# The delta rule's preparation and the first loads in another order, with six unread products ahead of the first group's scores

## The reference

```
x = x + 0.5 * swiglu(rmsnorm(x, ffn1_norm[i]), ffn1_w_gu[i], ffn1_w_down[i])     # i = 0 is the program's start
q, k, v = silu(conv4(h @ w_qkv));  q, k = unit(q) / sqrt(128), unit(k)           # mixer of layers 0 and 3
beta = sigmoid(h @ w_b);  g = -exp(a_log) * softplus(h @ w_a + dt_bias)
G = cumsum(g) inside each tile of 128 tokens                                     # 2 tiles, 8 heads of 128
L[i,j]  = beta[i] * exp(G[i] - G[j]) * (k[i] . k[j])   for j < i
QK[j,i] = exp(G[i] - G[j]) * (q[i] . k[j])             for j <= i
u = (I + L)^-1 (beta * (v - decayed k @ S));   o = decayed q @ S + QK^T u;   S = decayed S + k^T u
```

## Time and profile before

| | |
|---|---|
| median of the three runs | 3758.79 us (3758.35 to 3759.87) |
| the profiled execution: its time, its span | 3753.71 us, 3752.0 us |
| PE busy | 3662.1 us (98%) |
| DVE, ACT, POOL busy | 2248.1, 1474.3, 270.2 us |
| mean granted clock of PE | 0.993 |
| moved by DMA | 660.51 MB, 176 GB/s in the mean |

### The profile page before, as it was taken

The page is one execution under the profiler, slowest core; times in us unless marked ns, Lnnn a source line. Parts: engine busy times, 40 slices in busy tenths (PEclk is TensorE's granted clock), DMA queues, the critical chain, the costliest instruction groups (busy, mean ns, idle before and its releaser), DMA issues.

```text
span 3752.0 us, 47545 instructions
## 1 busy us (share of the span) xinstructions
PE 3662.1 (98%) x18612; PEld 3030.6 (81%) x18612; DVE 2248.1 (60%) x2973; ACT 1474.3 (39%) x1957; POOL 270.2 (7%) x322
## 2 busy tenths in 40 slices
PE   7998999999999999999998999999999999999999
PEld 6898788889788875888898788888888688888587
DVE  5777577774577755777776577555434555541254
ACT  3454244443434424444462344444311444431143
POOL 0003200000000001000013100000001100000000
PEclk9999999999999999999999999999999999999999
DMA  8652086764476744766640374645532254553452
GB/s 291 234 171 85 20 278 213 246 230 152 158 250 207 259 145 152 241 233 225 221 149 26 134 264 159 223 146 202 164 100 66 81 202 168 202 196 101 168 179 102
DMA packets 453529, 660.51 MB, mean 176 GB/s; under 512 B 15288, under 2 KB 385299, under 8 KB 452904
## 3 DMA queue, kind: packets, MB, share of 16 engines
q1 hardware_dynamic: 432280, 579.48, 45.5%
q0 software_dynamic: 21072, 78.56, 6.5%
HBM read 656.94 MB, written 2.00 MB: 176 GB/s over the span
## 4 chain that ended last, share of the span: by engine, by line
PE 92%; DVE 4%; ACT 2%; issue 1%; SPq 0%; POOL 0%; DMA 0%; POOLq 0%; ACTq 0%; DVEq 0%
PE ps L790 14%; PE ps L792 14%; PE ps L791 14%; PE ps L810 7%; PE ps L812 7%; PE ps L811 7%; PE ps L1137 4%; PE ps L3080 3%; PE ps L800 2%; PE ps L1551 1%; PE ps L2800 1%; PE ps L2803 1%; DVE parts L727 1%; PE ps L3077 1%; PE ps L1483 1%; PE ps L1484 1%
## 5 line engine op out<-in xcount | busy, mean ns | idle before, releaser
L727 DVE TENSOR_TENSOR parts<-ring,parts 128x2048 fp32r<-128x2048 f32 (+1 forms) x339 | 756.9, 2235 | 609.4 <-ACT parts L713 609.3
L790 PE MATMUL ps<-parts 128*128 128x512 f32 x2288 | 905.3, 396 | 0.5 <-DVE parts L998 0.3
L792 PE MATMUL ps<-parts 128*128 128x512 f32 x2288 | 891.8, 390 | 0.0
L791 PE MATMUL ps<-parts 128*128 128x512 f32 x2288 | 890.9, 389 | 0.0
L713 ACT ACTIVATE parts<-ring 128x2048 fp32r<-128x2048 f32 x330 | 630.6, 1913 | 569.1 <-PE ps L792 417.3
L792 PEld LDWEIGHTS ps<-parts 128*128 128x128 f32 x2288 | 429.4, 188 | 91.4
L790 PEld LDWEIGHTS ps<-parts 128*128 128x128 f32 x2288 | 429.9, 188 | 85.9 <-issue 1.7
L791 PEld LDWEIGHTS ps<-parts 128*128 128x128 f32 x2288 | 430.2, 188 | 84.8
L810 PE MATMUL ps<-parts 128*128 128x512 f32 x1144 | 450.3, 394 | 0.3
L812 PE MATMUL ps<-parts 128*128 128x512 f32 x1144 | 446.1, 390 | 0.0
L811 PE MATMUL ps<-parts 128*128 128x512 f32 x1144 | 445.2, 389 | 0.0
(11 more groups left out here) (433 smaller groups left out, 4443.3 us busy)
## 6 DMA issues: line engine op xcount, KB each, us to landing
ring<-in_ffn_w_gu SPq DMA_DIRECT2D x176, 1024.0 KB
ring<-in_ffn_w_in SPq DMA_DIRECT2D x110, 1024.0 KB
ring<-in_ffn_w_down SPq DMA_DIRECT2D x88, 1024.0 KB
ring<-in_ffn_w_out SPq DMA_DIRECT2D x55, 1024.0 KB
ring<-in_gdn_w_in SPq DMA_DIRECT2D x32, 1024.0 KB
arena<-in_w_mod POOLq DMA_DIRECT2D x24, 1024.0 KB, 6.0
xn<-in_w_mod POOLq DMA_DIRECT2D x24, 1024.0 KB, 7.7
arena<-in_w_mod POOLq DMA_DIRECT2D x48, 512.0 KB, 9.1
```

What stands on the lines that cost most here:

```text
L727: ins = nc.vector.tensor_tensor(lower, unit_raw(at, j)[:, sides_, :], upper, ALU.subtract)
L790: nc.tensor.matmul(dst, h_u, w_u[:, :, n, :], start=(k == 0), stop=False)
L791: nc.tensor.matmul(dst, h_u, w_l[:, :, n, :], start=False, stop=False)
L792: ins = nc.tensor.matmul(dst, h_l, w_u[:, :, n, :], start=False, stop=(k == KD - 1))
```

## The change

Two places change: the start, and the preparation of both delta rules. At the start, constants are cut in 320 columns that go first and 3168 that go after chunk 2; the 14 small loads go to ACT's queue ahead of everything else ACT does; the other six go on SP behind chunk 2; ACT splits its first two units before `rows_act`; DVE makes their lower parts before it waits for `gains_ready`; PE makes 9 unread products in place of 12; and in the first feed-forward the first chunk's `up` calls go by half, then tile (the semaphore counts in `unit_freed` and `sums_done` follow). In the delta rule, PE's, ACT's and DVE's orders change, spread 1 goes to bank 3, six unread products precede group 0, and values, the decayed k and the small product move in among the level updates.

```diff
-    def rows_sp(sp):
+    def gain_rows_act(act):
...
+    def rows_sp(sp):
...
+    def late_consts_sp(sp):
+        sp.dma_start(consts[:, C_EARLY:NCONST], A["consts"][:, C_EARLY:NCONST]).then_inc(consts_loaded, 16)
@@ rows_dve
-        dve.wait_ge(gains_ready, 6)
@@ ffn_sp
             ffn_load(sp, at, c)
+            if c == RING - 1 and at is PLACES[0]:
+                rows_sp(sp)
+                late_consts_sp(sp)
@@ ffn_pe
-                spin(12, 3)
+                spin(9, 3)
-        up(0, 1, 0)
-        up(0, 0, 1)
-        up(0, 1, 1)
+        for half, t in ((0, 1), (1, 0), (1, 1)) if at is PLACES[0] else ((1, 0), (0, 1), (1, 1)):
+            up(0, half, t)
@@ ffn_act
-            rows_act(act)
             for j in range(GU_SLOTS):
                 gu_upper_act(act, at, j)
+            rows_act(act)
@@ ffn_dve
             split_first_dve(dve, at)
+            dve.wait_ge(gains_ready, 6)
@@ gdn
+    SPREAD = [7, 3, 7, 6]
+    PREP_SPREAD, PREP_GROUP = [1, 2, 3, 6], [4, 5, 7, 8]
@@ gdn_pe
         spread(0)
+        spread(1)
         to_rows(0)
         to_rows(1)
         turn(NQKV - 1)
         to_rows(2)
         to_rows(3)
-        spread(1)
+        spread(2)
+        spin(6, 2)
+        group(0)
         for n in range(4, 8):
             to_rows(n)
-        spread(2)
-        group(0)
+        group(1)
         spread(3)
-        for g in range(1, 4):
-            group(g)
+        wide_level(*SCHED[0])
+        group(2)
+        group(3)
@@ gdn_act
         silu_of(NQKV - 1)
+        table("natural_log_exp_and_others")
         to_rows(1)
-        table("natural_log_exp_and_others")
+        decay(0)
+        decay(1)
...
-        decay(0)
         for n in range(4, 8):
             to_rows(n)
-        for g in range(1, 4):
-            decay(g)
+        decay(2)
+        decay(3)
@@ gdn_dve
-        differences(0)
-        differences(1)
...
-        values(0)
...
-        differences(2)
...
-        nc.vector.tensor_tensor(k0, k0, bc_last(g_kd, P), ALU.mult).then_inc(gdn_kd, 1)
+        for g in range(3):
+            differences(g)
         group(0)
+        group(1)
         differences(3)
-        values(1)
-
-        group(1)
         update(*SCHED[0])
         group(2)
         group(3)
-        for t, lv in SCHED[1:-1]:
+        for n, (t, lv) in enumerate(SCHED[1:-1]):
             update(t, lv)
+            if n == 1:
+                values(0)
+            if n == 3:
+                keys()
+            if n == 5:
+                values(1)
```

More of the change, by code:

```diff
@@ L79 @@
 C_UPPER = 320
+C_EARLY = C_UPPER
 C_LOWER = 448
@@ L527, in spin @@
             nc.tensor.matmul(ps[:, bank, (c % 4) * P:(c % 4 + 1) * P], ident, col(C_ONES), start=True, stop=True)
[L529 removed]
+    def gain_rows_act(act):
         r = 0
         for name, rows in (("ffn1_norm", 4), ("mix_norm", 4), ("ffn2_norm", 4)):
[L532 removed]
+            act.dma_start(gain_rows[r:r + rows, :], A[name]).then_inc(gains_loaded, 16)
             r += rows
[L534 to L536 removed]
+        act.dma_start(gain_rows[r:r + 6, :], A["norm_g_2"].rearrange("l j d -> (l j) d")).then_inc(gains_loaded, 16)
+        act.dma_start(gain_rows[18:19, :], A["c_2"]).then_inc(gains_loaded, 16)
+        act.dma_start(gain_rows[19:20, :], A["c_ctx_2"].rearrange("(a d) -> a d", a=1)).then_inc(gains_loaded, 16)
         for j in range(2):
[L539 removed]
+            act.dma_start(col_rows[0:96, j, :], A["gdn_conv"][j].rearrange("w (c p) -> (w c) p", p=P))\
                 .then_inc(gains_loaded, 16)
@@ L543, in rows_sp @@
                 A[name].rearrange("l (c p) -> (l c) p", p=P)
-            sp.dma_start(col_rows[r:r + v.shape[0], 0, :], v).then_inc(gains_loaded, 16)
+            act.dma_start(col_rows[r:r + v.shape[0], 0, :], v).then_inc(gains_loaded, 16)
+        for l in range(2):
+            act.dma_start(m_rows[0:NMOD, l, :], A["b_mod_2"][l].rearrange("(n p) -> n p", p=P))\
+                .then_inc(gains_loaded, 16)
+    def rows_sp(sp):
         for j in range(2):
@@ L550, in rows_sp, with wait_all_consts @@
         sp.dma_start(d_gk[:, :], A["dsa_kidx_norm"][0].partition_broadcast(P)).then_inc(rows_loaded, 16)
-        for l in range(2):
-            sp.dma_start(m_rows[0:NMOD, l, :], A["b_mod_2"][l].rearrange("(n p) -> n p", p=P))\
-                .then_inc(gains_loaded, 16)
+    def late_consts_sp(sp):
+        sp.dma_start(consts[:, C_EARLY:NCONST], A["consts"][:, C_EARLY:NCONST]).then_inc(consts_loaded, 16)
+    def wait_all_consts(eng, at):
+        if at is MIXERS[0]:
+            eng.wait_ge(consts_loaded, 32)
     def rows_pe(pe):
@@ L690, in unit_freed @@
             j += UNITS[at["kind"]]
-        first = at["kind"] in ("ffn", "gdn") and j < 2
+        first = at["kind"] in ("ffn", "gdn") and j < 2 and at is not PLACES[0]
         return 2 * at["unit"] + (3 + j if first else 2 * j + 2)
     def sums_done(at, b, t):
-        return 2 * at["unit"] + (2 + 2 * t if b == 0 else 4 * b + 3 + t)
+        return 2 * at["unit"] + (2 + 2 * t if b == 0 and at is not PLACES[0] else 4 * b + 3 + t)
     def count(n, it, step):
@@ L1313, in gdn_pe @@
     def gdn_pe(pe, at):
+        wait_all_consts(pe, at)
         j = at["n"]
@@ L1422, in group @@
                 pe.wait_ge(gdn_conv, NQKV * (j + 1))
+                pe.wait_ge(gdn_D, 4 * j + hg + 1)
             else:
@@ L1489, in merge @@
                 ins.then_inc(gdn_TV, 1)
-        for t, lv in SCHED[:-1]:
+        wide_level(*SCHED[0])
+        group(2)
+        group(3)
+        for t, lv in SCHED[1:-1]:
             wide_level(t, lv)
@@ L1718, in gdn_dve @@
     def gdn_dve(dve, at):
+        wait_all_consts(dve, at)
         j = at["n"]
@@ L1757, in differences @@
             cols = slice(8 * t + 4 * hg, 8 * t + 4 * hg + 4)
-            dve.wait_ge(gdn_prep, 8 * j + (g + 1 if g < 3 else 5))
-            step(dve, nc.vector.tensor_tensor(wide(g_V[:, g, :]), wide(ps[:, 7 - g % 2, :]), bc_last(g_gc[:, cols], P),
+            dve.wait_ge(gdn_prep, 8 * j + PREP_SPREAD[g])
+            step(dve, nc.vector.tensor_tensor(wide(g_V[:, g, :]), wide(ps[:, SPREAD[g], :]), bc_last(g_gc[:, cols], P),
                                               ALU.subtract))
@@ L1840, in gdn_dve, with keys @@
                     unit(1)
-        differences(0)
-        differences(1)
-        dve.wait_ge(gdn_tok, NQKV * (j + 1))
-        values(0)
-        dve.wait_ge(gdn_gates, 6 * j + 6)
-        step(dve, nc.vector.scalar_tensor_tensor(out=g_nb, in0=g_beta[:, 8:16], scalar=-1.0, in1=g_eg[:, 8:16],
-                                                 op0=ALU.mult, op1=ALU.mult))
-        differences(2)
-        dve.wait_ge(gdn_Tps, 8 * j + 4)
-        k0 = g_tok[:, 0, D:2 * D].rearrange("p (h d) -> p h d", d=P)
-        nc.vector.tensor_tensor(k0, k0, bc_last(g_kd, P), ALU.mult).then_inc(gdn_kd, 1)
+        def keys():
+            dve.wait_ge(gdn_gates, 6 * j + 6)
+            step(dve, nc.vector.scalar_tensor_tensor(out=g_nb, in0=g_beta[:, 8:16], scalar=-1.0, in1=g_eg[:, 8:16],
+                                                     op0=ALU.mult, op1=ALU.mult))
+            dve.wait_ge(gdn_Tps, 8 * j + 4)
+            k0 = g_tok[:, 0, D:2 * D].rearrange("p (h d) -> p h d", d=P)
+            nc.vector.tensor_tensor(k0, k0, bc_last(g_kd, P), ALU.mult).then_inc(gdn_kd, 1)
+        for g in range(3):
+            differences(g)
         group(0)
+        group(1)
         differences(3)
-        values(1)
-        group(1)
         update(*SCHED[0])
@@ L1902, in gdn_pool @@
     def gdn_pool(pool, at):
+        wait_all_consts(pool, at)
         j = at["n"]
@@ L3543, in _ @@
             ffn_load(sp, PLACES[0], 0)
-            rows_sp(sp)
             for at in STEPS:
@@ L3550, in _ @@
         def _(act):
+            gain_rows_act(act)
             for at in STEPS:
```

18 lines of the change are left out of this document (7 added, 11 removed).

## The result

The changed kernel takes 3733.09 us in the median of four runs (3728.74 to 3734.00). The kernel before, run beside it on the same chip, took 3759.24. The ratio is 0.9928, with a 95% interval of 0.9911 to 0.9946, so it is faster by 0.5 to 0.9%. The forecast was 3739.3 with a range of 3731.5 to 3750: the time lies in the range, and the gain (26 us) is larger than the one forecast (19.5).

The account below looks back on a forecast made before the run. The prediction took PE as the bound, 92% of the chain, with gains only where the chain leaves PE or PE's time is not work. Start 8.2 plus preparation 11.3 gave 19.5: 3758.8 - 19.5 = 3739.3 us, range 3731.5 to 3750.

Parts of the forecast that it names:

- The start: Program start: first read product at 22.6 in place of 30.8, 8.2 us off, from 5 (ACT held) to 9.
- Chunk 0: First weights at the start: last byte at 16.2, under h's last copy at 17.9, so they would not delay it.
- The preparation: Both delta rules, first spread to third merge: 5.7 us off in each, 11.3 in both.
- the clock's term: Delta rule preparation: two to three low-clock stretches of PE, 1.6 us each, counted as 4.1 us lost.
- 9.8 - 4.1: Each delta rule: 9.8 us won up to the third merge less 4.1 for low clock, giving 5.7.
- Both gaps that the sum had named: PE's idle gaps left in the first delta rule's preparation: 341.8 to 344.9, with 0.45 of work within, and 354.7 to 356.9.
- The moved DVE work: `values` and `keys` moved into the delta rule's level loop: cost nothing, levels staying 5.4 us apart.
- the median of the runs lies 5.1 above that execution: Whole program: 5.1 us from profiled execution to median, taking the forecast from 3734.2 to 3739.3.
- A: Rival: delta rule preparation gives its gain back through clock falls or delays; 3750.6 us, chance 0.11.
- B: Rival: the start gains nothing, bound by transfers or ACT held by its issues; 3747.5 us, chance 0.08.
- C: Rival: slower, low clock lasting from group 2 in both delta rules; 12.4 us slower, 3771, chance 0.03.
- D: Rival: both places hidden by a stream that fixes the end; 3758.8 +- 4 us, chance 0.04.

Follow-up runs that it names:

- e8: The changed kernel with the 14 small loads issued by SP behind chunk 0 instead of by ACT; 3731.31 us, ratio 0.9936 to the kernel before.
- e3: The changed kernel run once more, unchanged; 3731.79 us, ratio 0.9919 to the kernel before.
- e11: The changed kernel with level 0 of tile 0 on PE back behind groups 2 and 3; 3748.04 us, ratio 0.9976 to the kernel before.
- e12: The new start with the old preparation, only level 0 of tile 0 moved between groups 1 and 2; 3742.62 us, ratio 0.9960 to the kernel before.
- e2: The kernel before with the delta rule's new preparation alone, old start kept; 3742.27 us, ratio 0.9950 to the kernel before.
- e1: The kernel before with the new start alone, delta rules left as before; 3749.54 us, ratio 0.9969 to the kernel before.

## Why the prediction was right, point by point

**The start.** The sum's steps and what the trace of after has: x lands by 6.8 (1.32 and 5.5 to landing; forecast 6.4); ACT's first square 7.37 (7.5); second transposes end 17.13 (17.25); h's last copy 17.77 (17.9); small rows turned 18.88 (19.05); unread products end 22.80 (22.65); first read product 22.46, or 22.81 in the chain, from which the forecast was reckoned (22.6). The estimate of 0.38 us for an issue on ACT's queue, which no row of before showed, was good: 14 issues took 5.2 us, 0.37 each, and in the eleven traces that have them there they end between 6.0 and 6.9. The two ends that the forecast gave the start, 5 us with ACT held and 9, rest on issues that hold ACT much longer or cost it nothing; no run shows either, only those 5.1 to 6.0 us. Behind the start chunks 1 and 2 were complete at 26.5 and 42.1 (26 and 40); ACT waited 0.41 us for chunk 2, and PE had no gap above 0.1 us from the first read product to 215 us. Chunk 0 was the step that came nearest to failing. The forecast had it by 16.2, of which 0.7 us is for the small loads ahead of it. e8, where they stand behind it, has it only at 17.2, 1.7 later than that sum without them (15.5); in the changed kernel its last transfer reports at 17.87, and ACT begins on it at 17.89. So nothing was left of the 1.7 us of cover counted, and had the norms been faster, the weights would have set the start.

The Trainium skill says in "DMA: Bandwidth & Descriptors", section "Issuing engines are not separate DMA queues", that transfers started by several engines interleave on the same 16 DMA engines. The runs agree, with numbers for this case: x lands 5.5 us after its issue with the 14 loads on ACT's queue and 4.9 with them behind chunk 0 (e8), so in this pair 0.26 MB of small loads cost it 0.6; the prediction's estimate by that page was 0.7. From run to run it varies as much: with the 14 loads on ACT's queue and the constants cut x took 5.3 to 6.2 us, and ACT's issues and table load still set the first square.

One price was missing. By their distances the passes were slow during the unread products before, too, but by the time 24 were over they had become fast. With 18 they had not: the first three read products stand at 22.46, 23.03 and 23.46, and only from 23.87 on are they 0.23 us apart. From the first to the fourth it takes 1.41 us where it took 0.82 before, so this costs 0.6 us. The fourth product is 7.62 us sooner than before (31.49 and 23.87), and so is the first spread (7.68), short of the 8.21 at the first.

**The preparation.** The path was right at nearly each mark, and the size of the clock's term was not. Distances from the first spread, forecast and (measured in e3, which had no low clock before merge 1): group 0 7.9 (8.1), group 1 12.0 (12.2), group 2 18.3 (18.6), merge 1 24.1 (24.5), merge 3 33.6 at full clock (34.8 with one low stretch). I counted two to three low stretches in each delta rule, "4.1 us". The windows give 40 x 0.09 x 2 = 7.2 us at the low level in the first delta rule, two stretches, and 3.7 in the second, one. The marks give 6.4 and 7.6 us at merge 3, and 7.6 and 8.7 at the merge behind it (49.0 us from the spread before, 41.4 and 40.3 now), for the 5.7 forecast. So the stretches were one or two and not two or three, and 9.8 - 4.1 came out as 7.6 and 8.7. Both gaps that the sum had named did stay: 1.57 and 0.87 us with half a level between them ahead of PE's group 2, and 2.04 ahead of 351.25. Behind the first one the clock fell in this profile and in the second run of the same kernel (e3) it did not:

```profile
320.00:346.00 26.00, 20.90 (x176) 19.54 (x177) 20.31 (x30) 13.01 (x27) 6.66 (x5) 1.00 0.06 25
```

So at such a gap it is not settled beforehand whether the clock falls; before, at 3.16 us, it did in both delta rules.

Why the move pays is shown by e11 and e12: level 0 and its update run beside groups 2 and 3. The prediction had said so ("PE has behind it what came later before"). It left the size to a sum along the path; e11 shows that without that one move the whole preparation gains nothing (31.5 and 32.3 at merge 1 against 30.4), and e12 that the move alone does not make it either.

**The moved DVE work.** Forecast as harmless where it went, and it is: the levels stay 5.4 us apart. That POOL holds DVE up is seen in the rows above: a DVE product with both inputs in SBUF (L1802, at 340.92) takes 1.64 us beside POOL's 1.27, and 0.69 alone (333.15). The Trainium skill, "SBUF — State Buffer", section "Who interferes with whom", calls this an exclusive lock; the trace agrees. The moved pieces were not hit on the way to merge 3, but an update was, as before: the chain of waits of the changed kernel has a DVE instruction lengthened by 0.6 us, and PE's last eight products ahead of merge 3 start only behind it. In turn DVE held POOL up: beside `values` (352.98, 1.21 us) POOL's mask at 353.19 took 2.13 us, with no gap of PE behind it.

```profile
351.74 1.33 DVE xn L1814
...
353.20 1.95 PE ps L1489 x8
```

**The step that failed** is the last of the sum: "the median of the runs lies 5.1 above that execution". It was taken as an offset that both kernels share. It is not one: the changed kernel's median lies 0.2 above its profiled execution. The 5.1 us go with clock that the kernel before loses in most executions and did not lose in its profiled one (0.991 and 0.993), and the changed kernel has 0.994 in both. That PE's shorter gaps are the reason fits e11 and e12, which have long gaps and 0.992; no run shows it apart from the rest of the order. By the profiles alone the forecast of 19.5 stands against 20.8, and part of that closeness is luck: the marks give 24.0 (7.7 at the first spread, and 7.6 and 8.7 at the merges behind merge 3), and 3.2 of them are lost again elsewhere, which no step of the sum had. Most goes between the two delta rules: the second one's first spread is 10.0 us sooner (1965.23 for 1975.27), not 7.7 + 7.6 = 15.3. The trace of the changed kernel has four low stretches there, at 419.8, 843.0, 921.5 and 1860.2 us, that of the kernel before one, at 934.8. Behind the second delta rule 2.1 us come back.

**The rivals.** A (the preparation gives its gain back) fell with e2: 17.6 us by medians. B (the start gains nothing) fell with e1: 10.3 by medians, 7 to 16 by the ratio's interval. C (slower, the low clock lasts) is refuted by the windows: 0.93 and 0.96 in the stretches in question. D fell with the result.

## What to carry to other kernels

A reordering pays when it puts work with its inputs ready into the other engine's gap so that both run side by side; ask of each moved piece which engine stood idle for it before, and whether its own input is there early enough, or the move alone does nothing. Where PE's clock falls after its gaps, as it did here, a shorter gap can win more than its own length. Don't carry an offset between the profile and the median over to a kernel with other gaps: compare the mean granted clocks of the executions first. Unread products delay what stands behind them and may bring nothing for it, so run the kernel without them too.

## What the runs showed of the hardware

The time of one and the same kernel goes with its mean granted clock from execution to execution, 2.6 to 2.8 us for 0.001. The width of that scatter does not follow PE's gaps: the kernel before spreads over 8 to 12 us in its three groups and the changed one over 6, but e8 and the kernel with 17 unread products, which have the new preparation, over 12 and 15 in six executions each. A small issue on ACT's queue ahead of everything else cost ACT 0.25 to 0.57 us, and in the kernel before one cost SP 0.25 to 0.43. A later 1 MB issue on SP (4.64 in the changed kernel's timeline) took 4.28 us. And the windows view gives a clock of 1.00 for 20 to 24 us while the products' distance of 0.43 to 0.57 us, against 0.23 a little later, says that it was low: at the very start the distance is the better witness.
